# Attention over a paged latent cache: keys transposed in 32x32 blocks by VectorE, scores as 32x32 products on all tiles of TensorE

## The reference

```
s_past = (einsum('bqhc,bkc->bhqk', q_lat, c_past) + einsum('bqhr,bkr->bhqk', q_pe, kpe_past)) * MLA_SCALE
p = softmax(concat([s_past, s_new]))
out = einsum('bhqk,bkc->bqhc', p[..., :P], c_past) + einsum('bhqk,bkc->bqhc', p[..., P:], c_new)
```

## Time and profile before

| | |
|---|---|
| median of 3 runs | 1040.61 us (1038.58 to 1041.21) |
| the profiled execution, its own time | 1038.19 us |
| its span in the profile | 1036.3 us |
| PE busy | 983.4 us, 95% |
| DVE busy | 507.4 us, 49% |
| ACT busy | 445.6 us, 43% |
| POOL busy | 157.2 us, 15% |
| cache stage, first transpose to first product of W_out | 410.9 to 579.6 us |

### The profile page before, as it was taken

One profiled execution on the slowest core, in us unless ns is written; L12 is line 12 of the kernel. 1 busy time (PEld: TensorE's weight loads), 2 busy tenths in 40 slices (PEclk: granted clock), 3 DMA queues, 4 the chain that ended last, 5 costly groups with the idle time before them and its releaser, 6 DMA issues.

```text
span 1036.3 us, 20604 instructions
## 1 busy us (share of the span) xinstructions
PE 983.4 (95%) x8588; PEld 847.8 (82%) x8588; DVE 507.4 (49%) x991; ACT 445.6 (43%) x962; POOL 157.2 (15%) x257
## 2 busy tenths in 40 slices
PE   3999999999989999899999799999999999999997
PEld 3988899877757556566655799999999999999996
DVE  5456766665475385344444442633343234334423
ACT  6444638566646676344444433432232123213312
POOL 1020500255520201345541000000000000000000
PEclk8899969999999999899999899999999999999999
DMA  7222111130024600477772321422222222222302
GB/s 245 83 84 82 42 42 41 43 67 11 2 57 109 221 2 22 179 259 247 241 245 92 123 82 42 143 82 82 82 87 109 90 82 82 82 82 94 111 1 88
DMA packets 31655, 102.58 MB, mean 99 GB/s; under 512 B 14023, under 2 KB 14967, under 8 KB 25218
## 3 DMA queue, kind: packets, MB, share of 16 engines
q1 hardware_dynamic: 22346, 63.50, 18.6%
q0 software_dynamic: 9216, 37.75, 10.6%
HBM read 96.45 MB, written 4.22 MB: 97 GB/s over the span
## 4 chain that ended last, share of the span: by engine, by line
PE 87%; DVE 7%; ACT 4%; issue 2%; DMA 0%; SPq 0%; DVEq 0%; ACTq 0%
PE PS L585 17%; PE PS L587 17%; PE PS L586 17%; PE PS L1057 7%; PE PS L1068 3%; PE PS L1092 3%; PE PS L703 2%; PE PS L1075 2%; PE PS L775 1%; PE PS L806 1%; PE PS L858 1%; PE PS L958 1%; PE PS L567 1%; PE PS L677 1%; DVE SMX L2111 1%
## 5 line engine op out<-in xcount | busy, mean ns | idle before, releaser
L585 PE MATMUL PS<-XH,WH 128*128 128x272 f32 (+1 forms) x944 | 277.0, 293 | 4.0 <-DVE WL L1696 2.5
L587 PE MATMUL PS<-XH,WL 128*128 128x272 f32 (+1 forms) x944 | 276.2, 293 | 0.0
L586 PE MATMUL PS<-XL,WH 128*128 128x272 f32 (+1 forms) x944 | 275.3, 292 | 0.0
L585 PEld LDWEIGHTS PS<-XH,WH 128*128 128x128 f32 x944 | 180.1, 191 | 9.0 <-DVE WL L1696 4.2
L586 PEld LDWEIGHTS PS<-XL,WH 128*128 128x128 f32 x944 | 180.2, 191 | 0.0
L587 PEld LDWEIGHTS PS<-XH,WL 128*128 128x128 f32 x944 | 180.0, 191 | 0.0
L1201 ACT ACTIVATE WH<-RAW 128x2048 fp32r<-128x2048 f32 x47 | 89.9, 1914 | 204.5 <-PE PS L587 204.4
L585 PE MATMUL PS<-NH,WH 128*128 128x272 f32 x512 | 149.1, 291 | 0.8 <-DVE WL L1696 0.8
L587 PE MATMUL PS<-NH,WL 128*128 128x272 f32 x512 | 147.6, 288 | 0.0
L586 PE MATMUL PS<-NL,WH 128*128 128x272 f32 x512 | 146.6, 286 | 0.0
L1696 DVE TENSOR_TENSOR WL<-RAW,WH 128x2048 fp32r<-128x2048 f32 x47 | 107.9, 2297 | 63.1 <-ACT WH L1201 63.1
(11 more groups left out here) (315 smaller groups left out, 1443.8 us busy)
## 6 DMA issues: line engine op xcount, KB each, us to landing
RAW<-in_w_stream SPq DMA_DIRECT2D x47, 1024.0 KB, 4.8
XN<-in_hin SPq DMA_DIRECT2D x4, 512.0 KB, 6.0
out_y_p<-YO SPq DMA_DIRECT2D x4, 512.0 KB, 2.7
CST<-in_big SPq DMA_DIRECT2D x1, 1132.5 KB, 13.4
SS<-in_sstate SPq DMA_DIRECT2D x1, 1024.0 KB, 5.1
out_ssm_s<-SS SPq DMA_DIRECT2D x4, 256.0 KB
CN<-in_cache,IDX POOLq DMA_INDIRECT x64
WQN<-in_wq SPq DMA_DIRECT2D x3, 256.0 KB, 5.9
```

Of the source, the lines that this page charges most:

```text
L585: pe.matmul(PS[:, b, 0:n], wh, xh[:, k, c:c + n], start=(k == 0), stop=False)
L586: pe.matmul(PS[:, b, 0:n], wh, xl[:, k, c:c + n], start=False, stop=False)
L587: last = pe.matmul(PS[:, b, 0:n], wl, xh[:, k, c:c + n], start=False, stop=(k == DT - 1))
```

## The change

Five things change in the cache stage.

1. The nine groups of PE transposes, the nine copies out of PSUM, POOL's `pack_rope` and the tiles `KRN` go. DVE makes eight transposes for a chunk instead, SBUF to SBUF, each of which transposes every 32x32 block of its tile by itself: `CT[0][b]` takes the first 128 latent columns (4 blocks wide, 512 elements in each partition), `CT[1][b]` the other 160 with the rope columns (640 elements). There is one set of `CT`.
2. The scores become products of 32 rows and 32 columns of the array, with 128 moving columns: 9 blocks of columns (x) times 4 row strips (q) times 4 sequences (b), 144 for a chunk. Row strip q writes PSUM bank q, so one chunk's scores lie in four banks, 128 columns in each, and there is one set of them: `cache_scores(n, 0)` waits for the exponentials of chunk n - 1.
3. The queries must lie on every row strip. SP copies them there once, with 32 small DMAs (`QS` from `QF` and `QRF`), after `q_padded`.
4. DVE's steps for a running maximum become two instructions instead of four; ACT's second exponential comes behind the first. The reads of PSUM and the write of `PE_` take an access pattern with the four banks in it.
5. The orders: PE's loop is `cache_p(n - 1)`, the scores of n, `cache_values(n - 1)`. DVE transposes chunk n + 1 around the maximum of n and `accumulate(n - 1)`. DVE may transpose chunk 0 while the prompt's attention ends, and PE no longer waits for `po_copied` before its first scores. Values run one chunk behind the scores and not two, and POOL's gather of chunk n waits for `ce_pv` of n - 3.

The waits for some small loads are merged into fewer semaphores, with the same loads in the same order.

```diff
-            def cache_transposes(n, u):
...
-            def cache_scores(n, c):
...
+            def cache_scores(n, i):
+
+                if i == 0 and n >= 1:
+                    pe.wait_ge(sem("ce_exp"), n)
+                pe.wait_ge(sem("ct_done"), 8 * n + 4 * i + 4)
+                for x in range(4 + i):
+                    for q in range(4):
+                        rows = slice(32 * q, 32 * q + 32)
+                        for b in range(4):
+                            heads = slice(32 * b, 32 * b + 32)
+                            last = pe.matmul(PS[heads, q, 0:P], QS[rows, n // 8, 2 * x + i if x < 4 else 8, heads],
+                                             CT[i][b][rows, x, :, :].rearrange("p j k -> p (j k)"),
+                                             start=(i + x == 0), stop=(i == 1 and x == 4))
                 last.then_inc(sem("ct_used"), 1)
...
+            pe.wait_ge(sem("exp_done"), NS_)
+            pe.wait_ge(sem("qs_in"), 16 * 32)
+            for n in range(17):
+                if n >= 1:
+                    cache_p(n - 1)
+                if n < 16:
+                    cache_scores(n, 0)
+                    cache_scores(n, 1)
+                if n == 0:
+                    pe.wait_ge(sem("po_copied"), NT_)
+                if n >= 1:
+                    cache_values(n - 1)
...
+            def cache_transpose(n, i, b):
+                if i == 0 and b == 0:
+                    dve.wait_ge(sem(f"cn_in{n % 4}"), 64 * (n // 4 + 1))
+                if b == 0 and n >= 1:
+                    dve.wait_ge(sem("ct_used"), 2 * n - 1 + i)
+                src = CN[n % 4][b][:, :, P * i:P + (P + DR) * i]
+                dve.transpose(CT[i][b][:, :, :, :].rearrange("p x j k -> p j x k"),
+                              src.rearrange("p j (x c) -> p j x c", c=32)).then_inc(sem("ct_done"), 1)
...
+            for x in range(8):
+                cache_transpose(0, x // 4, x % 4)
+            for n in range(17):
+                if n + 1 < 16:
+                    for b in range(3):
+                        cache_transpose(n + 1, 0, b)
+                if n < 16:
+                    cache_max(n)
+                if n + 1 < 16:
+                    cache_transpose(n + 1, 0, 3)
+                    cache_transpose(n + 1, 1, 0)
+                if n >= 1:
+                    accumulate(n - 1)
+                if n + 1 < 16:
+                    for b in range(1, 4):
+                        cache_transpose(n + 1, 1, b)
...
+            sp.wait_ge(sem("dve_step"), DVE_STEP["q_padded"])
+            for q in range(4):
+                rows = slice(32 * q, 32 * q + 32)
+                for s in range(4):
+                    src = slice(32 * s, 32 * s + 32)
+                    sp.dma_start(QS[rows, :, 2 * s:2 * s + 2, :], QF[src, :, :, :]).then_inc(sem("qs_in"), 16)
+                    sp.dma_start(QS[rows, :, 8, src], QRF[src, :, src]).then_inc(sem("qs_in"), 16)
...
-            pack_rope(0)
-            pack_rope(1)
             pool.wait_ge(sem("pv_done"), NT_)
             gather(2)
             gather(3)
...
+            for n in range(4, 16):
+                pool.wait_ge(sem("ce_pv"), n - 3)
+                gather(n)
```

More of the change, by code:

```diff
@@ L307, in build @@
     assert cn_at[1][2] + rows_of <= w_at + 4 * DT * WC * 4
-    CT, at = [None] * 9, x_at
-    for i in range(9):
-        CT[i], at = put(f"CT{i}", [P, 512], F32, at)
+    CT, at = [[None] * 4, [None] * 4], x_at
+    for i in range(2):
+        for b in range(4):
+            CT[i][b], at = put(f"CT{i}_{b}", [P, 4 + i, 4, 32], F32, at)
     assert at <= x_at + 4 * 4 * (KV + DR) * 4
@@ L373, in build, with previous_max @@
         HALF0 = {"out": 10, "mlp": 18}
[L375 to L385, removed]
+        def previous_max(n):
+            return ML[:, n // 8, 0:1] if n % 8 == 0 else SME[:, (n - 1) % 3, 1:2]
         def gate_share(u):
@@ L1042, in _ @@
             prompt_values(NT_ - 1)
-            pe.wait_ge(sem("po_copied"), NT_)
-            def cache_transposes(n, u):
[L1048 to L1058, removed]
-            def cache_scores(n, c):
[L1062 to L1069, removed]
+            def cache_scores(n, i):
[5 more added lines that the diff above has]
+                        rows = slice(32 * q, 32 * q + 32)
+                        for b in range(4):
+                            heads = slice(32 * b, 32 * b + 32)
+                            last = pe.matmul(PS[heads, q, 0:P], QS[rows, n // 8, 2 * x + i if x < 4 else 8, heads],
+                                             CT[i][b][rows, x, :, :].rearrange("p j k -> p (j k)"),
+                                             start=(i + x == 0), stop=(i == 1 and x == 4))
                 last.then_inc(sem("ct_used"), 1)
[L1072 to L1076, removed]
             def cache_p(n):
@@ L2310, in _ @@
             gather(1)
-            def pack_rope(n):
-                if n >= 2:
-                    pool.wait_ge(sem("ct_mm"), 9 * (n - 1))
-                pool.wait_ge(sem(f"cn_in{n % 4}"), 64 * (n // 4 + 1))
-                for b in range(4):
-                    last = pool.tensor_copy(KRN[n % 2][:, :, b, :], CN[n % 4][b][:, :, KV:KV + DR])
-                last.then_inc(sem("kr_packed"), 1)
-            pack_rope(0)
-            pack_rope(1)
             pool.wait_ge(sem("pv_done"), NT_)
@@ L2324, in _ @@
             gather(3)
-            for n in range(2, 16):
-                if n >= 3 and n + 1 < 16:
-                    pool.wait_ge(sem("ce_pv"), n - 2)
-                    gather(n + 1)
-                pack_rope(n)
+            for n in range(4, 16):
+                pool.wait_ge(sem("ce_pv"), n - 3)
+                gather(n)
 def laid_out(x_prompt, x_sample, cache_latent, cache_krope, state_conv, state_ssm, page_table, meta_tokens,
```

106 lines of the change are left out of this document (35 added, 71 removed).

## The result

The changed kernel takes 1112.46 us (median of 4 runs, 1111.93 to 1113.3), the kernel before 1039.98 on the same chip: a ratio of 1.0698, with a 95% interval of 1.0684 to 1.0712. It is 7.0% slower, and the forecast was 995. The profiled execution took 1112.37, its span is 1110.6.

What follows compares the result with a forecast made beforehand. PE, busy without a gap, bound the cache stage. With its transposes gone, DVE would pace: chunk 0 to 419.6, 14 periods of 7.2 to 520.4, last chunk to 527.1 instead of 572.85; gain 46, so 995 us, range 984 to 1020.

Steps and rivals of the forecast that it cites:

- PE, for a chunk: PE's work in the cache stage: scores 2.0 us, transposes of the exponentials 0.46, values 1.73, with filling 4.9 us.
- the 7.2 of the forecast: Cache stage period: DVE never waits and paces each chunk at 7.2 us, ends 7.05 and 7.75; chance 0.60.
- the speedup on that page: PE's scores: sixteen tiles speed up 10.6 and not 16, so a step takes 0.33 us and the scores 2.9.
- The array: PE's score products: a step's 32 records of 128 columns take 0.216 us if all sixteen tiles overlap.
- The rival of the row strips: PE's scores: strips don't overlap with columns split, scores 7.8 us, period 10.4, 1043 us; chance 0.03 together with POOL.
- How the waits fit: Cache stage order: second scores done at 1.4 us, 0.4 of cover before DVE's maximum at 1.8, so DVE never waits.
- a dearer transpose: DVE's transposes cost more per element: loss above 1.7 times the price, chance 0.05; at twice, period 11.9, 1065 us.
- DVE and POOL blocking one another: Transposes beside POOL's gathers: 3.8 us added to DVE's, period 11, 1052 us; chance 0.03 together with strips.
- The clock: PE's new gaps in the cache stage halve its clock: 15 to 30 us more, 1010 to 1025; chance 0.20.

Runs made afterwards that it cites:

- the experiment: The kernel before with 72 added products of 4 columns (144 records) a chunk, ahead of the values instead of the first scores: 1099.8 us.
- with PE out of the way: The changed kernel with 64 score records a chunk instead of 288 and two idle products of 512 columns a chunk added, gathers kept: 1019.6 us.
- the run at the forecast's time: The changed kernel with 64 score records and two added idle products a chunk, without the gathers of chunks 4 to 15: 994.5 us.

## Why the prediction was wrong

**The step that failed** is in "PE, for a chunk": "Nine steps: 1.95 to 2.7 us. I take 2.0, because the 9.4 ns come from small columns on few tiles." The mis-sized term is issue: I took 2.0 us for 288 records, where the price of 9.4 ns for each would have made it 2.7. It measured 12.5 us in the chunk above, 43 ns for each record: 6.2 of records at 20 to 27 ns, 4.6 beside POOL's gathers, 1.8 at a fetch. The 9.4 ns were real (9.5 in 144 records of the experiment), but they held for 90 records with large products around them. The changed stage asks for 288 and their weight loads in each period, 648 instructions of PE with the rest where the old form had 180, and I multiplied a price from a short burst. Nor did I look at the instruction queue: its 8 packets in 100 us stand against 1863 instructions of PE, and the change made these 3.6 times as many for a chunk. With one fetch for 256 and never less than 3.2 us between two, 648 instructions need 8.1 us or more; that is an estimate from these runs. By it the 7.2 of the forecast was out of reach even without gathers, and the run with all records and no gathers took 10.0 us for a chunk.
The Trainium skill, "TensorE: Matmul & The Clock Gate", section "Measured speedup vs the span model", counts about 4 ns of issue for each tile. The trace shows more even for a short burst at full clock: 32 records start within 0.23 us, 7.5 ns apart. By the speedup on that page alone the scores would have stayed at 2.9 us, an estimate.

**The array** did as forecast at full clock. In a run whose 32 records were at hand they started within 0.23 us and took 0.50 in all, so sixteen tiles overlap, and half of the columns changed 1.6 us. The rival of the row strips is wrong. At half clock a burst does run slower with 128 columns than with 64, 22 ns a record against 15.

**How the waits fit** named the price: "were the scores later than that, all would be paid in full". In the chunk above the scores ended 9.8 us after DVE's last transpose (505.18 to 514.96) instead of 1.4, with 0.4 of cover. One premise fell with it: the first part of the scores didn't lie before that point but ended 4.2 us after it, so DVE's next transposes stood too, 26.8 of the 100 us.

**DVE** was right: the first chunk's eight transposes took 5.4 us (5.5 forecast), all 128 together 89.5. Its pace of 7.2 was 6.84 where nothing held it, and that run took 994.5. So the rivals of a dearer transpose and of DVE and POOL blocking one another are wrong too. The gathers kept 0.94 each.

**The clock** did fall, to 0.50 in about half of each period. The rival had priced it at 15 to 30 us on its own. With few records it cost 11; with all of them the slow supply makes the gaps, and the clock follows. In the kernel before, too, it fell from 1.00 to 0.73 when the 288 nearly empty records were added. It is a part of the loss and not its start.

**DMA**: with PE out of the way the stage moved 277 GB/s at a share of 0.81. In that run the data of a chunk had landed before DVE asked for them (488.8 against 491.1); but the transfers and the gathers' issuing made PE's small products slow: from 994.5 to 1019.6 even with 64 records.

Counted from the run at the forecast's time, the loss is: 994.5 to 1048.3 by the records alone, to 1093.5 with the transfers, to 1112.4 with POOL issuing them. The first of these steps also has the idle products taken out, so it holds some clock.

**What stays open.** That instructions arrive late is shown by their count, their place and the fetches. Why they do is not. For the transfers the packets' times are a hint. In the changed kernel a fetch falls in the last 2 us of every set's data. With plain transfers the fetches that ended pauses over 3 us started 3.9 to 7.0 us into the data and 6.3 to 9.0 after the fetch before, where the run without transfers had one every 3.9 on average. That is as if a fetch stood in line behind the data. But no run tests it, and beside POOL's issuing PE's own pace could put the fetches there too. What POOL's issuing shares with PE is open too; the signal that came 3.9 us late speaks for something wider than the fetch. And no version beat the kernel before with the complete computation.

## What to carry to other kernels

Before cutting a product into many small ones, count instructions: a price for each from a short burst holds only while PE has them at hand, so compare the instructions of a period with the packets of the instruction queue, and their distance with the 3.2 us that no run here went below. Expect several times the price when GpSimd issues gathers meanwhile. If the new work stands in a loop of two engines with little cover, price it from its worst row, not from its likeliest. When an engine idles for "issue", test by count against size: half the columns, then half the products; and put the suspected products, nearly empty, into the kernel that works.

## What the runs showed of the hardware

- One packet of 16 KB in the instruction queue for 256 added instructions of PE (233 to 274 in the 100 us windows), never two within 3.2 us. PE stood still for 0.7 to 5.3 us at such a packet. In six of the runs 58 pauses over 1.1 us between 425 and 640 are for "issue" and not beside POOL's issuing; each ended 1.2 to 1.6 us after such a packet.
- While POOL issued four indirect gathers (4.7 us), 41 to 52 records went through and then one to six every 0.7 to 0.8 us, until 0.9 to 1.1 us after the last gather's issue; with SyncE's plain transfers none was slow.
- A small fp32 product added to a full PE costs 85 to 92 ns (two records of 43 to 46); 52 where POOL isn't issuing; 106 when spread in eights.
- In a burst at half clock a record takes 15 ns with 4 or 64 columns on 32x32 tiles and 22 with 128 on sixteen of them; at full clock 9.5 with 4 and 15 with 128.
- The signal of the last product of a burst on 32x32 tiles came 3.9 us after its start beside gathers, 0.43 in the same kernel without.
- A 32x32 transpose of fp32 on DVE starts 0.59 to 0.64 us behind the last for 512 elements and 0.73 to 0.77 for 640, with and without gathers beside it.
- Products of 32-row and 128-row tiles don't overlap: 0.23 us at least for eight small products between large ones at full clock.
- The clock stood at 0.50 with PE counted as busy for 94%, when small tiles and narrow products alternated.
